# A mixture-of-experts block on Trainium2: blocks of 64 token slots with stationary weights, summed in DRAM by an accumulating scatter

## The reference, cut to what matters

```python
def _moe(h, router_w, router_b, w_gu, b_gu, w_down, b_down):
    T, D = h.shape                                   # 1024, 1024
    top_v, top_i = lax.top_k((h @ router_w + router_b).astype(jnp.float32), 4)
    gates = jax.nn.softmax(top_v, axis=-1)
    # 4096 (token, expert) pairs, sorted by expert and cut into blocks of one expert each
    def expert_block(xblk, e):
        gu = xblk @ w_gu[e] + b_gu[e]                # (rows, 1024) @ (1024, 2048)
        gate = jnp.minimum(gu[:, ::2], 7.0)
        up = jnp.clip(gu[:, 1::2], -7.0, 7.0)
        act = (up + 1.0) * gate * jax.nn.sigmoid(1.702 * gate)
        return act @ w_down[e] + b_down[e]           # (rows, 1024) @ (1024, 1024)
    # y[token] = sum over its 4 experts of gate * expert_block row
```

## Time and profile before

| | |
|---|---|
| runs of the kernel before, us | 3228.18 (median of 3; 3226.07 to 3236.08) |
| profiled execution, span from first to last instruction, us | 3229.3 |
| granted TensorE clock, mean | 0.950 |
| busy share of the span | PE 89%, PEld 50%, DVE 59%, ACT 52%, POOL 19% |
| blocks of 128 slots | 51 |
| DMA | 561.90 MB, mean 174 GB/s |

### The profile page before, as it was taken

The page is one execution under the profiler, slowest core; times in us unless marked ns, Lnnn a source line. Parts: engine busy times, 40 slices in busy tenths (PEclk is TensorE's granted clock), DMA queues, the critical chain, the costliest instruction groups (busy, mean ns, idle before and its releaser), DMA issues.

```text
span 3229.3 us, 46744 instructions
## 1 busy us (share of the span) xinstructions
PE 2889.6 (89%) x15280; PEld 1610.1 (50%) x15280; DVE 1919.0 (59%) x2476; ACT 1680.0 (52%) x2188; POOL 619.3 (19%) x558
## 2 busy tenths in 40 slices
PE   5699988989898985999989999999999999999982
PEld 2344558888887542444444444444444444444440
DVE  5734984443533447666686628766283686854856
ACT  5722534343443324555675537666364575655751
POOL 1201005353442001111111101111011111111115
PEclk8799999999999986999999999999999999999995
DMA  8500014000001317555896529786274696756966
GB/s 296 201 27 27 1 48 162 1 0 0 0 0 37 111 71 273 214 216 182 286 338 227 202 104 341 258 317 216 101 264 158 232 326 251 270 183 217 346 223 236
DMA packets 256340, 561.90 MB, mean 174 GB/s; under 512 B 9552, under 2 KB 10708, under 8 KB 256288
## 3 DMA queue, kind: packets, MB, share of 16 engines
q1 hardware_dynamic: 232320, 483.36, 41.7%
q0 software_dynamic: 13792, 44.76, 3.9%
q10 hardware_dynamic: 10176, 33.11, 2.7%
HBM read 743.78 MB, written 56.49 MB: 248 GB/s over the span
## 4 chain that ended last, share of the span: by engine, by line
PE 59%; DVE 20%; issue 10%; ACT 4%; DMA 3%; POOL 2%; DVEq 1%; POOLq 0%; ACTq 0%; SPq 0%; PEld 0%
PE ps L1615 11%; PE ps L1785 10%; PE ps L1787 10%; PE ps L1786 10%; DVE weights L1365 8%; PE ps L1741 4%; PE ps L1528 2%; PE ps L1529 2%; PE ps L1530 2%; ACT weights L950 2%; DMA hT<-in_w_gu_dram 2%; DVE qkv L1412 1%; PE ps L1664 1%; DVE qkv L1407 1%; DVE weights L1047 1%
## 5 line engine op out<-in xcount | busy, mean ns | idle before, releaser
L1785 PE MATMUL ps<-weights,qkv 128*128 128x512 f16 x2448 | 940.3, 384 | 77.8 <-DVE qkv L1421 77.6
L1786 PE MATMUL ps<-weights,qkv 128*128 128x512 f16 x2448 | 937.2, 383 | 0.0
L1787 PE MATMUL ps<-weights,qkv 128*128 128x512 f16 x2448 | 936.8, 383 | 0.0
L1365 DVE SCALAR_TENSOR_TENSOR weights<-hT,weights 128x4096 f16<-128x4096 f32 x128 | 565.7, 4421 | 143.8 <-ACT weights L950 143.2
L950 ACT ACTIVATE weights<-hT 128x4096 f16<-128x4096 f32 x128 | 462.1, 3611 | 88.7 <-DMA hT<-in_w_gu_dram 84.1
L1785 PEld LDWEIGHTS ps<-weights,qkv 128*128 128x128 f16 x2448 | 240.6, 98 | 388.0 <-DVE qkv L1421 85.4
L1787 PEld LDWEIGHTS ps<-weights,qkv 128*128 128x128 f16 x2448 | 241.6, 99 | 295.3 <-issue 11.2
L1786 PEld LDWEIGHTS ps<-weights,qkv 128*128 128x128 f16 x2448 | 241.5, 99 | 252.7 <-issue 8.4
L1407 DVE TENSOR_SCALAR qkv<-ps 128x256 f32<-128x256 f32 x204 | 85.6, 420 | 367.4 <-PE ps L1787 367.4
L1615 PE MATMUL ps<-weights 128*128 128x128 f32 x2240 | 285.1, 286 | 8.6 <-ACT weights L872 5.7
L1365 DVE SCALAR_TENSOR_TENSOR weights<-qkv,weights 128x4096 f16<-128x4096 f32 x64 | 282.6, 4416 | 15.7 <-ACT weights L950 15.7
(11 more groups left out here) (321 smaller groups left out, 3884.9 us busy)
## 6 DMA issues: line engine op xcount, KB each, us to landing
hT<-in_w_gu_dram SPq DMA_DIRECT2D x153, 2048.0 KB
qkv<-in_w_gu_dram SPq DMA_DIRECT2D x51, 2048.0 KB
hT<-in_w_down_dram SPq DMA_DIRECT2D x51, 2048.0 KB
qkv<-in_w_down_dram SPq DMA_DIRECT2D x51, 2048.0 KB
y_scratch<-qkv ACTq DMA_DIRECT2D x51, 512.0 KB, 4.1
weights<-in_w_ada_dram SPq DMA_DIRECT2D x12, 2048.0 KB, 8.6
y_scratch<-weights SPq DMA_DIRECT2D x1, 16384.0 KB, 44.1
qkv<-in_w_in_dram SPq DMA_DIRECT2D x4, 2048.0 KB, 8.1
```

What stands on the lines that cost most here:

```text
L1365: dve.scalar_tensor_tensor(wl[j], stage[j % 3].rearrange("p (k n) -> p k n", k=KD), WSCALE, wh[j], ALU.mult, ALU.subtract).then_inc(e_lo.s ...
L1785: pe.matmul(dst, h[:, k, :], wh[j][:, k, :], start=start, stop=False)
L1786: pe.matmul(dst, h[:, k, :], wl[j][:, k, :], start=False, stop=False)
L1787: return pe.matmul(dst, l[:, k, :], wh[j][:, k, :], start=False, stop=stop)
```

## The change

Counted from the router's choices for these inputs, 32 experts hold from 2 to 438 of the 4096 pairs. In blocks of 128 they make 51 blocks; in blocks of 64 they make 82: nine experts have one block of 64, ten have two, eight have three, and the others 4, 5, 6, 7 and 7.

- **Blocks of 64 slots, weights stationary.** The weight halves (128x128 pieces) become the stationary operand and the block's 64 columns the moving one. Gate/up is computed transposed, in 8 row pieces of 1 MiB (`GK`), 8+8 output strips of 128 features, 3 passes: 384 products of 64 columns; down in 4 pieces of 1 MiB (`DK`): 192 products. The activated block needs no transpose before down; the down result is transposed back (8 transposes, `turn_y`).
- **Order of the loop.** In turn t PE does gate/up of block t+1, `turn_y(t-1)` in between, the transposes of x for block t+2, then down of block t. DVE does `swiglu(t)`, the low halves of down for block t, the low halves of gate/up for block t+2. ACT: sigmoid(t), high half of the activation, high halves of down(t), `scale_y(t-1)`, high halves of gate/up(t+2), `copy_xT(t+2)`, `copy_yT(t)`. PE's gate/up of block t+1 waits for `s_gr` = t+1, that is, for `swiglu(t)` to have read PSUM. Both PSUM banks and both sets of weight halves are single.
- **SwiGLU** is done once a block on 128x512 elements, with the bias added by DVE from a transposed table; the bias product on PE and its DMA go.
- **h2** (scale and shift applied) is computed in row layout before the transposes, cut into f16 halves (ACT, POOL) and stored as `h2_scratch`; the gather then brings both halves, and `xT` is one copy.
- **The sum.** `y_scratch` has one row for each token (and 64 spare ones for empty slots). It starts as the product of gates and `b_down`, computed and stored ahead of the loop; ACT scales each block's rows with their gates (`gtab`), and POOL adds them in DRAM with an indirect DMA that accumulates, one a block. The end loads four pairs of tiles instead of gathering.
- **One-hots** are written eight columns at a time; a second product makes the table of gates.

```diff
@@ loop on SP
+            def load_gate_up(t):
+                e, new = block_of(t)
+                for k in range(GK):
+                    reached(sp, s_glo, t, GK, k - 3)
+                    sp.dma_start(gstage[k % 4], w_gu[0, bass.ds(e, 1), k * P:(k + 1) * P, :].rearrange("a p n -> p (a n)"),
+                                 cond=new > 0).then_inc(s_gst[k % 4], 16)
...
+            with sp.Fori(1, MAXB) as t:
+                with sp.If(t <= nprev):
+                    load_down(t)
+                    load_gate_up(t + 2)
@@ loop on POOL
+            def scatter(t):
+                reached(pool, s_ys, t, 16, 0)
+                pool.tensor_copy(idx[:, 1:2], slots[:, bass.ds(t, 1)]).then_inc(s_iy, 1)
+                pool.wait_ge(s_iy, t + 1)
+                pool.wait_ge(s_yc, t + 1)
+                pool.sem_inc(s_idle, 1)
+                pool.indirect_dma_start(out=y_d, out_offset=bass.IndirectOffsetOnAxis(ap=idx[:, 1:2], axis=0),
+                                        in_=ysb[0:B, :], in_offset=None, bounds_check=SEQ + B - 1, oob_is_err=True,
+                                        compute_op=ALU.add).then_inc(s_ys, 16)
...
+                    gather(t + 2)
+                    low_act(t)
+                    scatter(t - 1)
@@ loop on ACT
+            def high_gate_up(t, k):
+                act.wait_ge(s_gst[k % 4], t * 32 + (16 * (k // 4) + 16))
+                reached(act, s_gu, t, GK, k + 1 - GK)
+                act.activation(ghi[k], gstage[k % 4].rearrange("p (f b) -> p b f", b=2), ACT.Copy,
+                               scale=WSCALE).then_inc(s_ghi, 1)
...
+            def scale_y(t):
+                act.wait_ge(s_ty, t + 1)
+                reached(act, s_ys, t, 16, 0)
+                act.activation(ysb[0:B, :], ps[0:B, BY:BY + 2, :].rearrange("p b c -> p (b c)"), ACT.Copy,
+                               scale=gtab[:, bass.ds(t, 1)]).then_inc(s_yc, 1)
...
+                    sigmoid(t)
+                    high_act(t)
+                    next_down(t)
+                    scale_y(t - 1)
+                    next_gate_up(t + 2)
+                    copy_xT(t + 2)
+                    copy_yT(t)
@@ loop on DVE
+            def low_gate_up(t, k):
+                dve.wait_ge(s_ghi, t * GK + (k + 1))
+                dve.scalar_tensor_tensor(glo[k], gstage[k % 4].rearrange("p (f b) -> p b f", b=2), WSCALE, ghi[k],
+                                         ALU.mult, ALU.subtract).then_inc(s_glo, 1)
...
+            def swiglu(t):
...
+                dve.wait_ge(s_gu, t * GK + GK)
...
+                chain(dve.tensor_tensor(gate_n, gate, bias[:, bass.ds(e * 16, 8)].unsqueeze(2).to_broadcast([P, 8, B]), ALU.add))
+                dve.tensor_scalar(gate_n, gate_n, LIMIT * WSCALE, None, ALU.min).then_inc(s_gc, 1)
+                dve.tensor_tensor(up_n, up, bias[:, bass.ds(e * 16 + 8, 8)].unsqueeze(2).to_broadcast([P, 8, B]),
+                                  ALU.add).then_inc(s_gr, 1)
...
+                    swiglu(t)
+                    next_down(t)
+                    next_gate_up(t + 2)
@@ loop on PE
+            def gate_up(t, k):
+                pe.wait_ge(s_glo, t * GK + (k + 1))
+                if k == 0:
+                    pe.wait_ge(s_xc, t + 1)
+                    reached(pe, s_gr, t, 1, 0)
+                for b, bk in enumerate((BG, BU)):
+                    for f in range(8):
+                        dst, c = ps[:, bk, f * B:(f + 1) * B], slice(f * P, (f + 1) * P)
+                        first, end = k == 0 and f == 0, k == GK - 1
+                        pe.matmul(dst, ghi[k][:, b, c], xT[:, 0, k, :], start=first, stop=False, skip_group_check=True)
+                        pe.matmul(dst, ghi[k][:, b, c], xT[:, 1, k, :], start=False, stop=False, skip_group_check=True)
+                        last = pe.matmul(dst, glo[k][:, b, c], xT[:, 0, k, :], start=False, stop=end, skip_group_check=True)
+                last.then_inc(s_gu, 1)
...
+            with pe.Fori(1, MAXB) as t:
+                with pe.If(t <= nprev):
+                    for k in range(2):
+                        gate_up(t + 1, k)
+                    turn_y(t - 1)
+                    for k in range(2, GK):
+                        gate_up(t + 1, k)
+                    turn_x(t + 2)
+                    down(t)
```

More of the change, by code:

```diff
@@ new lines, in low_act @@
+            def low_act(t):
+                pool.wait_ge(s_ah, t + 1)
+                pool.tensor_tensor(al, act_n, ah, ALU.subtract).then_inc(s_al, 1)
+            gather(0)
+            for n in range(NT):
+                pool.wait_ge(s_yev, n + 1)
+                pool.dma_start(y_d[n * P:(n + 1) * P, :], yin[:, n % 2, :]).then_inc(s_yin[n % 2], 16)
+            gather(1)
+            gather(2)
+            low_act(0)
+            for i in range(2):
+                pool.wait_ge(s_yin[i], 16 * NT // 2)
@@ new lines, in _ @@
+            with pool.Fori(1, MAXB) as t:
+                with pool.If(t <= nprev):
+                    gather(t + 2)
+                    low_act(t)
+                    scatter(t - 1)
+                    pool.sem_inc(s_idle, 1)
+            low_act(nlast)
+            scatter(nprev)
+            scatter(nlast)
+            for n in range(1, NT, 2):
+                pool.wait_ge(s_scl, n // 2 + 1)
+                pool.wait_ge(s_x1l, 16 * NT)
+                pool.tensor_tensor(x1r[:, n, :], acc[:, n, :], x1r[:, n, :], ALU.add).then_inc(s_finp, 1)
@@ new lines, in high_down, with next_gate_up @@
+            def high_down(t, j):
+                act.wait_ge(s_dst[j], t * 16 + 16)
+                reached(act, s_dn, t, 2, 0)
+                act.activation(dhi[j], dstage[j].rearrange("p (j n) -> p j n", j=2), ACT.Copy,
+                               scale=WSCALE).then_inc(s_dhi, 1)
+            def next_gate_up(t):
+                with act.If(flag(t) > 0):
+                    for k in range(GK):
+                        high_gate_up(t, k)
+                with act.Else():
+                    act.wait_ge(s_ghi, t * GK)
+                    act.sem_inc(s_ghi, GK)
@@ new lines, in next_down, with copy_xT @@
+            def next_down(t):
+                with act.If(flag(t) > 0):
+                    for j in range(DK):
+                        high_down(t, j)
+                with act.Else():
+                    act.wait_ge(s_dhi, t * DK)
+                    act.sem_inc(s_dhi, DK)
+            def copy_xT(t):
+                act.wait_ge(s_tx, t + 1)
+                reached(act, s_gu, t, GK, 0)
+                act.activation(xT, ps[:, BX, :].bitcast(F16).rearrange("p (j k t) -> p j k t", j=2, k=KD),
+                               ACT.Copy).then_inc(s_xc, 1)
@@ new lines, in _ @@
+            for n in range(NT):
+                act.wait_ge(s_bd, n + 1)
+                if n >= 2:
+                    act.wait_ge(s_yin[n % 2], 16 * (n // 2))
+                act.activation(yin[:, n % 2, :], ps[:, 6:8, :].rearrange("p b c -> p (b c)"), ACT.Copy).then_inc(s_yev, 1)
+                if n < 6:
+                    high_gate_up(0, n + 2)
+            for i in range(2):
+                act.wait_ge(s_yin[i], 16 * NT // 2)
+            act.wait_ge(s_gtp, 2)
+            next_gate_up(1)
@@ new lines, in _ @@
+            copy_xT(1)
+            sigmoid(0)
+            high_act(0)
+            for j in range(DK):
+                high_down(0, j)
+            next_gate_up(2)
+            copy_xT(2)
+            copy_yT(0)
+            with act.Fori(1, MAXB) as t:
+                with act.If(t <= nprev):
+                    sigmoid(t)
[5 more added lines that the diff above has]
+                    copy_yT(t)
@@ new lines, in _ @@
+            dve.wait_ge(s_bguT, 3)
+            nprev = dve.value_load(meta[0:1, N_AT:N_AT + 1], min_val=MINB - 2, max_val=MAXB - 2)
+            nlast = nprev + 1
+            dve.wait_ge(s_gtp, 1)
+            dve.tensor_copy(gtab, ps[0:B, 7, 0:NB]).then_inc(s_gtp, 1)
+            for k in range(GK):
+                low_gate_up(0, k)
+            next_gate_up(1)
+            swiglu(0)
+            for j in range(DK):
+                low_down(0, j)
+            next_gate_up(2)
+            with dve.Fori(1, MAXB) as t:
+                with dve.If(t <= nprev):
+                    swiglu(t)
+                    next_down(t)
+                    next_gate_up(t + 2)
@@ new lines, in _ @@
+            turn_x(2)
+            down(0)
+            with pe.Fori(1, MAXB) as t:
[7 more added lines that the diff above has]
+                    down(t)
+            turn_y(nprev)
+            down(nlast)
+            turn_y(nlast)
+            pe.wait_ge(s_gr, nlast + 1)
```

814 lines of the change are left out of this document (376 added, 438 removed).

## The result

Median after 3446.05 us (3437.93 to 3448.84) against 3228.39 us before: a ratio of 1.066, 95% interval 1.064 to 1.068. The change makes the kernel 6.6% slower. The profiled execution spans 3436.0 us; forecast were 3375, so the sign and the stage are as predicted and some 60 us of the sum were missing.

The account below looks back on a forecast made before the run. PE and DVE were taken as nearly balanced before, with conversion stalling PE after the change. First gate/up at 1271, 50 to the loop, 2001 in it, 12 for the last block, 42 at the end: 3376, predicted as 3375 us; eight-of-ten range 3250 to 3590.

Parts of the forecast that it names:

- PE finishes down(t) and stands while a new expert is converted: Loop: PE idle about 10 us before gate/up, released by DVE's second bias sum, when block t+2 brings a new expert.
- The product: PE in the loop: each 64-column product with its own weight load takes 28.5 ns, between ends of 26.6 and 46.9.
- The rival of loads that aren't hidden: PE in the loop: weight load and columns add up to 46.9 ns a product, about 3930 us in all; chance 0.08.
- The 81 ns of the Trainium skill: PE: a documented distance of load and product pairs at 128 columns, giving 46.7 us a block and about 5300 in all.
- The pieces: Conversion of one weight piece in the loop: 2.3 us for DVE's low half, 1.9 us for ACT's high half.
- Kinds of turn: Loop turns: nothing new 18.3 us, down new 20.5, gate/up of t+2 new 30, both 37; sum 1936 us.
- The clock's 65 us: Loop: 3.1 us lost to PE's lower clock after a pause, 21 times, added to the sum of the turns.
- Ahead of the loop: Stage before the first block: first gate/up at 1271 us, with 23.5 us for eight tiles of gates times b_down.
- Blocks 0 and 1: Between first gate/up and the loop: 14 us for a low-clock gate/up, then a turn with both new: 50 us.
- the end: Stage after the last block, from yT to the last store: 42 us, a gain of 58 on 99.6.
- Scatter and fetch: Loop: a scatter landing at 18 us or 2 us a turn of instruction fetch adds 150, giving 3525 us; chance 0.14.
- the order of DVE's list: Loop: DVE's SwiGLU reads queue behind eight low halves of a new gate/up, so PE stands some 11 us.

Follow-up runs that it names:

- experiment 2: Changed kernel with no new experts after block 0 and 32 instead of 64 columns in each of a block's 576 products: 2791.3 us, one run.
- experiment 7: Changed kernel with the eight tiles of gates times b_down ahead of the first block written to two PSUM bank pairs in turn: 3435.4 us, one run.
- experiment 3: Changed kernel with the loop's end taken from the number of blocks instead of a constant 95 with a condition inside: 3446.23 us, five runs.
- Experiment 4: Changed kernel with DVE's reads of gate/up(t+1) moved between the second and third low half of block t+2: 3434.1 us, 1.062 of before.
- experiment 1: Changed kernel with the table of new experts zero after block 0, so no weights are loaded or converted in the loop: 2942.7 us, one run.
- 8: Lists as in 5, but DVE doesn't wait for ACT's counts where block t+2 brings no new expert: 3314.6 us, 1.025 of before.
- 9: ACT's list as in 6, but DVE doesn't wait for ACT's counts where block t+2 brings no new expert: 3485.6 us, one run.
- experiment 12: As experiment 11, with POOL's gather issued one block ahead, before the activations' low half: 3187.6 us, 0.986 of before.
- 5: Changed kernel with DVE's gate/up reads and ACT's copies of xT and yT moved between the conversions of block t+2: 3464.9 us, 1.072 of before.
- 6: Changed kernel with only ACT's copies of xT and yT moved between its high halves of block t+2: 3814.1 us, 1.180 of before.
- 10: As 8, with SwiGLU and both activation halves of block t+1 done in turn t, and the b_down tiles of experiment 7: 3409.3 us, 1.054 of before.
- experiment 11: As 10, with DVE giving all eight counts at once ahead of SwiGLU and ACT's second cut moved from six to five: 3218.3 us, 0.9955 of before.

## Why the prediction came out as it did

- **Rows first, sum second.** The claim that PE finishes down(t) and stands while a new expert is converted holds: 472 us of PE's idle time with the releaser named ahead of time.
- **The product**, 28.5 ns: 29.2 to 29.3. The rival of loads that aren't hidden is out by experiment 2. The plain block: 18.3 forecast, 18.8 at full clock. The 81 ns of the Trainium skill ("TensorE: Matmul & The Clock Gate", section "Back-to-back issue gap") are shown by no run here, at 16, 32 or 64 columns.
- **The pieces**: DVE 2.3, measured 2.29; ACT 1.9, measured 1.90 for down and 2.07 for gate/up, whose source is read with a step of two. I had kept a tenth as the other end; it was that end.
- **Kinds of turn.** Forecast 18.3 / 20.5 / 30 / 37, measured 19.9 / 19.8 / 31.9 / 38.7. Against the forecast that is 30 x 1.6 = +47, 19 x -0.7 = -13, 19 x 1.9 = +36, 11 x 1.7 = +19. The clock's 65 us, which I had added apart, are inside the measured turns. Net +24: a plain turn behind a pause is 1.3 to 2.5 us longer than at full clock, not the 3.1 read from the earlier trace rows, and the chain of eight pieces is 2 us longer than put together from its parts. These are the terms that were mis-sized in the loop, in both directions, and the sum hid it: 2004 for 79 turns, where 1980 were forecast. That it came so near is in part luck. The clock behind the pause that ends at 1418.86:

```profile
1418.90:1421.00 2.10, 2.10 (x41) 2.10 (x42) 1.66 (x3) 0.20 (x1) 0.00 (x0) 0.50 0.00 0
1423.00:1425.00 2.00, 2.00 (x53) 1.99 (x50) 0.00 (x0) 0.75 (x1) 0.00 (x0) 1.00 0.00 0
```

- **Ahead of the loop** lies a miss of 20 us, second to the loop's 24: first gate/up at 1291.2 for 1271. (The 1260 that the prediction gives for the kernel before is the border of a stretch; that kernel's first gate/up product starts at 1253.4. The split into parts used it, the total did not.) The tiles with b_down took 4.9 us each for 3.0: I had taken ACT as their bound and PE's f32 products as hidden, and they run at a clock of 0.50, one behind the other with the copy (experiment 7). Together 37.5 us for 23.5, 14 of the 20. The last router product came at 1210.9 for 1205, the other 6.
- **Blocks 0 and 1** 54 us for 50; **last blocks** 40.4 for 32.5, for which the 14 empty turns, 9.5 us and not in my sum at all, account (experiment 3); **the end** 46.6 for 42.
- Together 20 + 4 + 24 + 8 + 5 = 61 of the 60 between 3376 and 3436.
- **Scatter and fetch**: ACT waited for a scatter once, and the instruction queue moved 43 packets, 0.70 MB, in the whole execution, so the long loop body isn't fetched each turn. Both rivals are out, but for the pauses of up to 0.6 us a turn of the last section, whose cause is open.
- **Where the reason was too narrow.** I put the stall down to "the order of DVE's list". Experiment 4 says no: with DVE's list changed, 398 of the 472 us stay, on ACT. The cause is a ring: ACT's list, DVE's list, the counts that free the staging buffers and POOL's gather each hold PE or the next conversion back, and each shows only once the one that comes later in time is gone. What was also missing is that the count of a block that converts nothing decides when the next expert's loads start.

## What to carry to other kernels

Where an engine's list holds a long job for the next item in front of a short one that another engine waits for, cut the long job and put the short one in; but go through all in-order lists that feed the same wait, SP's and POOL's included, before judging by a run. When a wait has gone and the time hasn't, read who releases it now. A branch that does nothing still gives counts: give them first, and don't make them wait for work that doesn't exist.

## What the runs showed of the hardware that I had not expected

The plain turn has two lengths, 18.8 and 19.2 to 19.5 us, by kernel, and nearly the same in each such turn of one kernel. The difference is two pauses of PE of 0.26 to 0.41 us from start to start at 64 columns (0.51 to 0.57 at 32), behind about the 219th and the 475th PE record of a turn, some 256 apart, in which PE waits for nothing that the trace shows. The second, from experiment 1:

```profile
1805.54 0.19 PE L1911 MATMUL ps<-qkv,weights 128*128 128x64 f16 x1
1805.57 0.19 PE L1909 MATMUL ps<-qkv,weights 128*128 128x64 f16 x1
1805.87 0.19 PE L1910 MATMUL ps<-qkv,weights 128*128 128x64 f16 x1
```

Experiments 1 to 4, 8, 9 and 12 have them, the changed kernel and 5, 6, 7, 10 and 11 don't. PE's own list is the same in experiment 1 and the changed kernel, where one DVE instruction differs, and the same in experiments 11 and 12, where POOL's order and one wait of ACT differ. So it isn't what PE computes; that it is where the program lies in memory fits, but no run here tests it. It is worth up to 0.6 us x 79 = 47 us where no turn waits for anything else, as in experiment 1, 12 us in experiment 12, and 5 of the 9.5 us that experiment 3 had won. Of two kernels that differ by under 2%, this has to be looked at before the difference is explained.

Also: POOL's low half of the activations lasts longer beside DVE's conversions. In experiment 11 it took 2.86 to 3.02 us in all 31 blocks where it fell beside low halves on DVE, and 1.15 to 1.16 in the 51 others. One of each:

```profile
1389.81 3.02 POOL L705 TENSOR_TENSOR qkv<-qkv 128x512 f16<-128x512 f32 x1 [12.29 <-ACT qkv L1039]
1408.38 1.16 POOL L705 TENSOR_TENSOR qkv<-qkv 128x512 f16<-128x512 f32 x1 [6.59 <-ACT qkv L1039]
```
